# The first two jobs of a float32 kernel take x without its norm, and the operand is normed in place during the second

## What is computed

```python
def rmsnorm(x, g):
    xf = x.astype(jnp.float32)
    y = xf * lax.rsqrt(jnp.mean(jnp.square(xf), axis=-1, keepdims=True) + NORM_EPS)
    return (y * g.astype(jnp.float32)).astype(x.dtype)

        h = rmsnorm(x, g[0])
        proj = h @ w_in[l]
        (u_pool, u_conv, c_gate, b_gate_conv, q, k, v, qi, ki, wi) = jnp.split(proj, pts, axis=-1)
```

## Time and profile before

| | |
|---|---|
| median of 3 runs | 2202.75 us |
| the profiled execution | 2202.97 us |
| its span in the trace | 2201.2 us |
| TensorE busy | 2192.6 us |
| VectorE busy | 1508.8 us (69%) |
| ScalarE busy | 1066.5 us (48%) |
| GpSimd busy | 63.2 us (3%) |

### The profile page before, as it was taken

One profiled execution on the slowest core, in us unless ns is written; L12 is line 12 of the kernel. 1 busy time (PEld: TensorE's weight loads), 2 busy tenths in 40 slices (PEclk: granted clock), 3 DMA queues, 4 the chain that ended last, 5 costly groups with the idle time before them and its releaser, 6 DMA issues.

```text
span 2201.2 us, 37987 instructions
## 1 busy us (share of the span) xinstructions
PE 2192.6 (100%) x16122; PEld 2064.7 (94%) x16122; DVE 1508.8 (69%) x1910; ACT 1066.5 (48%) x1418; POOL 63.2 (3%) x72
## 2 busy tenths in 40 slices
PE   9999999999999999999999999999999999999998
PEld 9999999999999889989988988988889999999987
DVE  7899588888889657544554555555766656576776
ACT  5454445544444646444443443444656555444443
POOL 1000000000000000000000000000100000010001
PEclk9999999999999999999999999999999999999999
DMA  8876676787787656555656556656664445688784
GB/s 275 246 240 203 199 249 227 225 276 258 258 285 259 230 176 193 190 199 184 202 194 193 187 200 203 194 195 203 227 201 144 135 147 169 219 270 288 253 279 156
DMA packets 248034, 475.00 MB, mean 216 GB/s; under 512 B 21526, under 2 KB 26000, under 8 KB 247096
## 3 DMA queue, kind: packets, MB, share of 16 engines
q1 hardware_dynamic: 243032, 454.40, 64.1%
q0 software_dynamic: 4832, 18.16, 2.5%
HBM read 468.30 MB, written 5.78 MB: 215 GB/s over the span
## 4 chain that ended last, share of the span: by engine, by line
PE 99%; issue 0%; DVE 0%; ACT 0%; POOLq 0%; POOL 0%; DVEq 0%
PE ps L891 21%; PE ps L892 21%; PE ps L893 21%; PE ps L884 11%; PE ps L886 11%; PE ps L885 11%; PE ps L808 1%; PE ps L905 0%; PE ps L675 0%; PE ps L797 0%; PE ps L720 0%; PE ps L707 0%; PE ps L787 0%; PE ps L788 0%; PE ps L786 0%
## 5 line engine op out<-in xcount | busy, mean ns | idle before, releaser
L891 PE MATMUL ps<-op0h,whiW 128*128 128x256 f32 x3376 | 936.9, 278 | 0.0
L893 PE MATMUL ps<-op0h,wloW 128*128 128x256 f32 x3376 | 932.3, 276 | 0.0
L892 PE MATMUL ps<-op0l,whiW 128*128 128x256 f32 x3376 | 932.2, 276 | 0.0
L1282 DVE TENSOR_TENSOR wloW<-raw,whiW 128x1024 fp32r<-128x1024 f32 (+1 forms) x503 | 610.8, 1226 | 336.5 <-ACT whiW L938 334.4
L938 ACT ACTIVATE whiW<-raw 128x1024 fp32r<-128x1024 f32 (+1 forms) x504 | 529.0, 1058 | 577.8 <-PE ps L893 474.0
L891 PEld LDWEIGHTS ps<-op0h,whiW 128*128 128x128 f32 x3376 | 633.7, 188 | 2.2 <-issue 1.3
L892 PEld LDWEIGHTS ps<-op0l,whiW 128*128 128x128 f32 x3376 | 633.8, 188 | 0.5
L893 PEld LDWEIGHTS ps<-op0h,wloW 128*128 128x128 f32 x3376 | 633.7, 188 | 0.0
L1282 DVE TENSOR_TENSOR wloT<-raw,whiT 128x1024 fp32r<-128x1024 f32 (+1 forms) x264 | 317.5, 1212 | 249.3 <-ACT whiT L938 248.0
L938 ACT ACTIVATE whiT<-raw 128x1024 fp32r<-128x1024 f32 (+1 forms) x264 | 273.8, 1047 | 290.8 <-PE ps L886 243.8
L884 PE MATMUL ps<-whiT,op1h 128*128 128x512 f32 x640 | 249.2, 389 | 0.0
(11 more groups left out here) (308 smaller groups left out, 2061.8 us busy)
## 6 DMA issues: line engine op xcount, KB each, us to landing
raw<-in_w_in SPq DMA_DIRECT2D x256, 512.0 KB, 4.5
raw<-in_w_up SPq DMA_DIRECT2D x128, 512.0 KB, 3.8
raw<-in_w_down SPq DMA_DIRECT2D x128, 512.0 KB, 4.0
raw<-in_w_ada SPq DMA_DIRECT2D x96, 512.0 KB, 4.6
raw<-in_w_gate SPq DMA_DIRECT2D x96, 512.0 KB, 5.0
raw<-in_w_out SPq DMA_DIRECT2D x64, 512.0 KB, 4.6
raw<-in_w_branch SPq DMA_DIRECT2D x48, 512.0 KB, 4.7
raw<-in_w_proj_a SPq DMA_DIRECT2D x24, 512.0 KB, 5.5
```

The costliest lines, as they stand in the source:

```text
L891: pe.matmul(o, wh, xh[:, ka, :], start=first and m % 2 == 0, stop=False, skip_group_check=True)
L892: pe.matmul(o, wh, xl[:, ka, :], start=False, stop=False, skip_group_check=True)
L893: mm = pe.matmul(o, wl, xh[:, ka, :], start=False, stop=last, skip_group_check=True)
L1282: v.tensor_tensor(wlo[job.mode][q % NSPL][:, :, 0:job.n], x, h.bitcast(F32), ALU.subtract).then_inc(s_lo, 1)
```

## The change

1. x is loaded in four blocks of 512 columns, all tokens in each. Block 0 goes first, blocks 1 to 3 stand between the weight loads of chunks 1, 2, 3 and 4. The two small vector loads move to ACT's queue. POOL's loads no longer stand behind the `rstd` of x.
2. PE transposes x as loaded. `qi0` and `qi1` run on the operand without the token's factor. Of the zero matmuls ahead of x 4 are left of 12, and 0, 2 and 2 stand where 4, 1 and 1 stood.
3. The row sums (`x0_square`, `x0_var`) become side work of steps 4 and 5. DVE then scales the identity by the token's factor (`x0_diagonal`, step 7), PE multiplies it by ones so that every partition holds all 256 factors (`x0_spread`, before chunk 8), and DVE copies that to `spread` (step 9).
4. The results of `qi0` and `qi1` are multiplied by `spread` as DVE reads them (`scale_qi`, steps 9 and 17), where ACT and DVE copied half each.
5. During `qi1`, once chunk 8 + p has read pair p of the operand, POOL adds its high and low part and multiplies by `spread` (two instructions of 128x512), ACT writes the new high part (`x0_high`, step 10 + p) and DVE the new low part (`x0_low`, step 11 + p). There are 8 pairs and two buffers, `tmp[2]` and `tmp[3]`, so that POOL's pair p waits for `x0_low` of p - 2. `kk` waits for its pairs.
6. The first ada group moves from chunk 10 to chunk 13; the number of early groups stays 13, so that the last is at chunk 56, where it was at 53.

```diff
-        for q in (list(range(of["qi1"].first + 2, of["vw"].first, 3)) + list(range(of["pool0"].first, NQ, 3)))[:13] + ...
+        for q in (list(range(of["qi1"].first + 5, of["vw"].first, 3)) + list(range(of["pool0"].first, NQ, 3)))[:13] + ...
...
+        for tt in range(2):
+            side(act_at, 4 + tt, "x0_square", tt)
+            side(dve_at, 4 + tt, "x0_var", tt)
+        side(dve_at, 7, "x0_diagonal")
+        side(pe_at, 8, "x0_spread")
+        side(dve_at, 9, "x0_spread")
+        side(dve_at, 9, "scale_qi", 0)
+        side(dve_at, 17, "scale_qi", 1)
+        for p in range(8):
+            side(act_at, of["qi1"].first + 2 + p, "x0_high", p)
+            side(dve_at, of["qi1"].first + 3 + p, "x0_low", p)
...
+        spread, diagonal, ones = tmp[4][:, 0:256], tmp[4][:, 256:512], tmp[5][:, 128:256]
...
-            for t in range(2):
-                sp.dma_start(x0[:, t, :], rows_of("x", t)).then_inc(s_x[t], 16)
+            def columns_of_x(j):
+                sp.dma_start(x0[:, :, 512 * j:512 * j + 512], x_columns[:, :, 512 * j:512 * j + 512]).then_inc(s_x[j], 16)
+
+            columns_of_x(0)
...
             for i, (kind, m) in enumerate(loads):
-                if i == 4:
+                if 2 <= i <= 4:
+                    columns_of_x(i - 1)
+                if i == 5:
...
-            rstd("x0", 0)
-            rstd("x0", 1)
             pool.wait_ge(s_raw[0], 16)
...
+            rstd("x0", 0)
+            rstd("x0", 1)
             pool.wait_ge(s_erow_v, 1)
...
+            pool.wait_ge(s_rb, 1)
+            for p in range(8):
+                x = half(tmp[2 + p % 2])
+                pool.wait_ge(s_pe, of["qi1"].first + p + 1)
+                if p >= 2:
+                    pool.wait_ge(s_xnop, p - 1)
+                pool.tensor_tensor(x, op0h[:, 2 * p:2 * p + 2, :].bitcast(F32), op0l[:, 2 * p:2 * p + 2, :].bitcast(F32), ALU.add).then_inc(s_xsum, 1)
+                pool.wait_ge(s_xsum, p + 1)
+                pool.tensor_tensor(x, x, spread.unsqueeze(1).broadcast_to([128, 2, 256]), ALU.mult).then_inc(s_xn, 1)
...
+            def x0_spread():
+                pe.wait_ge(s_ones, 1)
+                pe.wait_ge(s_diag, 1)
+                pe.wait_ge(s_oper, 8)
+                pe.matmul(bank[6][:, 0:256], ones, diagonal, start=True, stop=True).then_inc(s_spread, 1)
...
+                elif job.name == "kk":
+                    pe.wait_ge(s_xnop, k // 2 + 1)
...
-            warm(12)
+            warm(4)
...
-            warm(4)
             turn_x(0)
-            warm(1)
+            warm(2)
             turn_x(1)
-            warm(1)
+            warm(2)
...
+            def x0_high(p):
+                act.wait_ge(s_xn, p + 1)
+                act.activation(op0h[:, 2 * p:2 * p + 2, :], half(tmp[2 + p % 2]), ACT.Copy).then_inc(s_xnhi, 1)
...
+            def x0_diagonal():
+                v.wait_ge(s_rstd, 2)
+                for tt in range(2):
+                    op = v.tensor_scalar(diagonal[:, 128 * tt:128 * tt + 128], ident[:, :], norm_col("x0", tt)[1], None, ALU.mult)
+                op.then_inc(s_diag, 1)
...
+            def scale_qi(n):
+                job = of[f"qi{n}"]
+                v.wait_ge(s_pe, job.end)
+                for i, b in enumerate(pair_of(job)):
+                    c = 4 * n + 2 * i
+                    v.tensor_tensor(qb[:, c:c + 2, :], half(b), spread.unsqueeze(1).broadcast_to([128, 2, 256]), ALU.mult).then_inc(s_pair[job.pair], 1)
+
+            def x0_low(p):
+                v.wait_ge(s_xnhi, p + 1)
+                v.tensor_tensor(op0l[:, 2 * p:2 * p + 2, :], half(tmp[2 + p % 2]), op0h[:, 2 * p:2 * p + 2, :].bitcast(F32), ALU.subtract).then_inc(s_xnop, 1)
```

More of the change, by code:

```diff
@@ L86, in blk @@
         return [(c0, 512)]
-    jobs = [Job("qi0", "W", "x0", w_in, blk(5632), "copy", fresh=True),
-            Job("qi1", "W", "x0", w_in, blk(6144), "copy"),
+    jobs = [Job("qi0", "W", "x0", w_in, blk(5632), "qi", fresh=True),
+            Job("qi1", "W", "x0", w_in, blk(6144), "qi"),
             Job("kk", "W", "x0", w_in, [(5120, 256), (6656, 64), (6656, 64)], "kk"),
@@ L155, in program @@
         n = 0
-        for q in (list(range(of["qi1"].first + 2, of["vw"].first, 3)) + list(range(of["pool0"].first, NQ, 3)))[:13] + list(range(of["q0"].first + 2, NQ, 3))[:51]:
+        for q in (list(range(of["qi1"].first + 5, of["vw"].first, 3)) + list(range(of["pool0"].first, NQ, 3)))[:13] + list(range(of["q0"].first + 2, NQ, 3))[:51]:
             ada_after[q].append(n)
@@ L425, in program @@
         s_const = sem("pool_constants")
-        s_x = [sem(f"x_rows{i}") for i in range(2)]
+        s_x = [sem(f"x_columns{i}") for i in range(4)]
         s_va, s_vb, s_ident = sem("vectors_a"), sem("vectors_b"), sem("ident")
@@ L1351, in turn_x, with x0_var, x0_spread @@
                 v.tensor_tensor(l, x, h.bitcast(F32), ALU.subtract).then_inc(s_oper, 1)
+            def x0_var(tt):
+                part, (ss, rs), x = col("x0_parts")[:, tt:tt + 1], norm_col("x0", tt), x0[:, tt, 1024:2048]
+                for j in (2, 3):
+                    v.wait_ge(s_x[j], 16)
+                v.tensor_tensor_reduce(junk0[:, 1024:2048], x, x, 1.0, D * EPS, ALU.mult, ALU.add, ss).then_inc(own.sem, own.up())
+                v.wait_ge(own.sem, own.n)
+                v.wait_ge(s_sumsq, tt + 1)
+                v.tensor_scalar(rs, part, ss, 1.0 / D, ALU.add, ALU.mult).then_inc(s_var, 1)
+            def x0_diagonal():
[3 more added lines that the diff above has]
+                op.then_inc(s_diag, 1)
+            def x0_spread():
+                v.wait_ge(s_spread, 1)
+                v.tensor_copy(spread, bank[6][:, 0:256]).then_inc(s_rb, 1)
+                v.wait_ge(s_rb, 1)
+            def scale_qi(n):
[7 more added lines that the diff above has]
+                v.tensor_tensor(op0l[:, 2 * p:2 * p + 2, :], half(tmp[2 + p % 2]), op0h[:, 2 * p:2 * p + 2, :].bitcast(F32), ALU.subtract).then_inc(s_xnop, 1)
             def vectors_b(step):
@@ L1601, in fourier_d @@
                 v.tensor_tensor(op1l[:, 12 + g, :], tmp[5][:, 0:256], op1h[:, 12 + g, :].bitcast(F32), ALU.subtract).then_inc(s_four, 1)
-            parts = {"vectors_b": vectors_b, "bias_row": bias_row, "index_sum": index_sum, "top_rounds": top_rounds, "pool_window": pool_window, "pool_low": pool_low, "conv_taps": conv_taps,
+            parts = {"x0_var": x0_var, "x0_diagonal": x0_diagonal, "x0_spread": x0_spread, "scale_qi": scale_qi, "x0_low": x0_low, "vectors_b": vectors_b, "bias_row": bias_row, "index_sum": index_sum, "top_rounds": top_rounds, "pool_window": pool_window, "pool_low": pool_low, "conv_taps": conv_taps,
                      "softmax1_max": softmax1_max, "softmax1_scale": softmax1_scale, "values1": values1, "fold_map": fold_map, "ada_quarters": ada_quarters,
```

106 lines of the change are left out of this document (46 added, 60 removed).

## The result

The changed kernel takes 2222.34 us (median of 6 runs, 2220.05 to 2223.01), the kernel before, run beside it, 2202.74: a ratio of 1.0087, 95% interval 1.0075 to 1.0098. The forecast was 2220.0, with 2206 to 2227 as its range. The profiled execution took 2222.61.

What follows compares the result with a forecast made beforehand. TensorE, busy for 2192.6 of 2201.2 us, was taken as the bound. The terms -4.35 + 1.7 + 2.2 + 16.6 + 1.1 = +17.25, on a profiled 2202.97, gave 2220.2, median 2220.0; range 2206 to 2227.

Steps and rivals of the forecast that it cites:

- D: Norming the operand in place, chunk 9 to 24: GpSimd and VectorE exclude each other, so TensorE waits; +16.6 us.
- GpSimd 20.6: Chunk 9 to low part 20: GpSimd's 16 instructions at 1.29 us, 20.6 us, added in full to VectorE's work.
- the rival without exclusion: During `qi1` and `kk`: both engines overlap and a loop over pairs costs 5.0 us, in all 2208.4; chance 0.17.
- The rival with VectorE alone yielding: Same stretch: GpSimd overlaps what VectorE has begun, only VectorE yields at length; about 10 us, in all 2213; no chance given.
- A: The start: chunk 0 begins at 8.6 us for 12.95, a gain of 4.35 us.
- busy from 1.18 on: At the start: TensorE works from 1.18 us, at half rate until 7.1, then at the full rate.
- the stated bound of 10.0: Start of chunk 0 if TensorE's rate stays half that long: gain 2.95 us.
- B: Loads, chunks 3 and 4: GpSimd's earlier loads slow SP's queue, so weights land late; +1.7 us.
- the fallen clock: Rival: behind the gaps ahead of chunks 16 to 20 TensorE runs at half rate; 2223 or 2226 us; chance 0.14.
- C: The spread factor: TensorE waits for `x0_diagonal` ahead of chunk 8; +2.2 us.
- the bound named as 0.4: Lower bound for the spread factor's cost ahead of chunk 8: 0.4 us.
- E: The last early ada group at chunk 56: more VectorE work where it has little slack, ahead of chunk 67; +1.1 us.

Runs made afterwards that it cites:

- experiment 1: The changed kernel without the norming in place (GpSimd's 16 instructions, `x0_high` and `x0_low` left out): 2207.62 us.
- experiments 2 and 3: The first is under experiment 2; the second is the kernel before with 16 GpSimd fills of 128x512 in place of that one's instructions: 2202.90 us, ratio 0.9999.
- experiment 4: The changed kernel with four buffers in place of two for GpSimd's results: 2222.81 us; then also `x0_high` and `x0_low` two steps later: 2218.02 us.
- experiment 2: The kernel before, with GpSimd adding and multiplying 128x512 in SBUF eight times each during `qi1`, results unused there: 2212.24 us, ratio 1.0043.
- experiment 6: The changed kernel with GpSimd's loads behind weight chunk 4 instead of chunk 0: 2218.35 us; then also six zero matmuls first and an earlier table load: 2218.39 us.
- the busy start: The changed kernel with GpSimd's loads later, six zero matmuls for four ahead of the vector transpose, and ScalarE's table load earlier: 2218.39 us.
- the mended kernels: The changed kernel with norming on VectorE, later GpSimd loads, busier start, ada groups moved, `x0_spread` before chunk 9: 2203.44 us; late groups and second `scale_qi` moved too: 2200.28 us.
- experiment 7: The changed kernel with twelve early ada groups in place of thirteen, the last at chunk 53, and one more at chunk 251: 2221.62 us.
- two steps later: The changed kernel with four buffers for GpSimd's results and `x0_high` and `x0_low` each two steps later: 2218.02 us.
- ada groups behind `vw`: The changed kernel with norming on VectorE and the four ada groups of chunks 13 to 22 taken out, four more standing late: 2218.87 us.

## Why the prediction was right, and where it was off

The forecast missed the median by 2.3 us, and came that near partly by luck: its errors go both ways, between the terms and inside the largest.

- **D, +16.6 for +14.97.** The mechanism was right: GpSimd's instructions and VectorE's with two inputs in SBUF do not run together, and this alone costs 8.9 us (experiments 2 and 3); with the norming left out D is 0 (experiment 1). But the size is right by two errors that go against each other. The step held VectorE for all of "GpSimd 20.6", and in the trace it is held for about 8: an instruction of GpSimd's costs a busy VectorE 1.04, not 1.29, and beside an idle one nothing. And the step took VectorE to be always at work, where it is idle for 11.2 us, waiting behind ScalarE's `x0_high` for GpSimd's results: the loop over two buffers was worth 1.6 of D and the order in the queues 2.7 (experiment 4). So the rival without exclusion had a part of the truth in its loop, and falls by experiment 2. The rival with VectorE alone yielding falls too: GpSimd's additions take up to 2.74 us. The Trainium skill's rule ("Who interferes with whom") held, except that the loser does not block for the whole of the other's 1.29 us.
- **A, -4.35 for -2.34.** The step "busy from 1.18 on" failed: the four zero matmuls are over at 5.0, and the gate biases, which the step had landing in time, came at 5.8. This is the stated bound of 10.0, and 0.6 more. ScalarE's table load (1.28 us at 6.78) was not in the step; in the kernel before it lay under the wait for x. The rate stayed half until past 9.5 in this trace, and not in the three named under experiment 6, whose chunk 0 is at 9.5. The term itself was also misread: a start gained ahead of a late load is no gain, since chunk 4 stood between 25.6 and 26.1 in the seven traces with GpSimd's loads early, with chunk 0 anywhere from 9.5 to 10.9.
- **B, +1.7 for +4.10.** The load itself was late by 2.5 (chunk 4 at 26.02 with chunk 0 at 10.58; 23.65 in experiment 6). The step let SP's queue run at 0.13 MB/us for 7 us, at the full rate behind, and chunk 4 land at 19.9; it landed at 22.8. The queue from 10 to 23 us in the profile after (packets, MB, share):

```profile
q1 hardware_dynamic: 1669, 2.89, 62.9%
```

  That is 0.22 MB/us for 13 us: slowed less, and for longer. From 11 to 18 us it got 1.65 MB, where the step had 0.9, and from 18 to 23 us 0.84 MB, 0.17 MB/us, where the step had the full rate. The other 1.56 is the fallen clock, which the forecast had as a rival, but behind the later gaps. There it costs nothing in this trace, and in others what the rival said: 2.9 us with four buffers and 2.8 with the busy start, 1.0 to 1.7 in three more. (The rival's 2226 is a slip: 2222.9 and the 1.4 of A's upper bound are 2224.3.) The Trainium skill, "TensorE: Matmul & The Clock Gate", "The HAM clock gate", states that the array falls back when it idles; ahead of chunk 4 it did so in four of seven traces.
- **C, +2.2 for +1.56.** Right in kind: TensorE waits ahead of `x0_spread`, for 0.9 us where the step had 1.8. With the spread matmul one chunk later the mended kernels pay 0.3 for it (chunk 8 to 9 in 3.05 for 2.72), the bound named as 0.4.
- **E, +1.1 for +1.07**, and experiment 7 gives it back to the hundredth in the trace. The place was only in part the one named: 0.4 comes ahead of chunk 67, and 0.7 at 188.8 us, where TensorE waits for `pool_window` behind the same group. The size was luck to that extent.

The terms measured add up to 19.35, and 0.3 more comes behind chunk 99: 19.6, the difference of the spans. Against the forecast's 17.25, A and B brought 4.4 more, and C and D 2.3 less.

## What to carry to other kernels

Before work goes to GpSimd because it is idle, add its time to VectorE's in that stretch, if GpSimd reads SBUF and VectorE has two inputs there; if the sum is over the time at hand, the cheaper place is VectorE itself (6 us here). A head start is worth only what the next late load leaves of it, so price start and loads as one term. A small instruction that waits for a slow engine should stand behind, not ahead of, the work that feeds the critical engine in the same queue (2.7 us here).

## What the runs showed of the hardware

- GpSimd and VectorE with two inputs each in SBUF mostly alternate: in experiment 2 a multiply-add every 1.70 us in place of 0.66. But at times GpSimd waited behind several. In the run with four buffers and later places an addition began at 66.33 and was done at 71.15, with six of VectorE's beside it, five of them at their usual length. What decides between the two is open:

```profile
66.33 4.82 POOL L589 TENSOR_TENSOR nb<-op0h,op0l 128x512 f32<-128x512 f32 x1 [2.62 <-DVE op0l L1428]
```

- VectorE's multiplication of a 128x512 tile in SBUF by a column is held too: two of them took 2.96 us beside GpSimd in that run, 0.87 in the trace after.

```profile
49.63 2.96 DVE L1349 TENSOR_SCALAR tmp<-raw,csil 128x512 f32<-128x512 f32 x2
```

- GpSimd's fills of 128x512 (0.53 us) are free beside VectorE.
- TensorE's granted clock fell to 0.5 behind waits of 2.3 to 2.7 us ahead of chunk 4 in four of the traces (after, four buffers, norming on VectorE, last group at 53) and stayed whole in three with waits of 1.7 to 2.4 (no norm, two steps later, ada groups behind `vw`). What decides it is open. It costs 1.5 to 1.6 us each time, and behind chunk 20 up to 2.9. The runs of the changed kernel are 3.0 us apart, while those of the kernel before, in which TensorE never waits behind its first matmul, agree within 0.1%; that the clock makes this difference was not tried.
